# The layer norm of the convolution between the last value tiles, and the sample's convolution taps multiplied on ScalarE

## What is computed

```python
h = _rmsnorm(x, norm_mix_g)
q, k, v, iq, ik, iw, glu, ga, gc = jnp.split(h @ w_in, splits, axis=-1)
# branch A: selected sparse attention, 8 heads of 64; prompt and sample
attn_out = attention(q, k, v, iq, ik, iw, cache) @ w_attn_out
# branch B: convolution
ga_in, gb_in = jnp.split(glu, 2, axis=-1)
u = ga_in * jax.nn.sigmoid(gb_in)
u_full = jnp.concatenate([past_conv, u], axis=1)
c = causal_depthwise_conv(u_full, conv_dw_w)          # 31 taps, 512 channels
c = jax.nn.silu(_layernorm(c + conv_dw_b, conv_ln_g, conv_ln_b))
conv_out = c @ w_conv_out
x = x + (jax.nn.sigmoid(ga) * attn_out + jax.nn.sigmoid(gc) * conv_out) @ w_out
x = x + (jax.nn.silu(h2 @ w_ffn_gate) * (h2 @ w_ffn_up)) @ w_ffn_down   # h2 = rmsnorm(x)
```

## Time and profile before

| | us |
|---|---|
| median of 3 runs | 1997.33 |
| the profiled execution | 1996.86 |
| its span | 1995.1 |
| PE busy | 1872.1 (94%) |
| DVE busy | 1094.6 (55%) |
| ACT busy | 766.1 (38%) |
| POOL busy | 261.0 (13%) |

### The profile page before, as it was taken

How to read it: one execution, slowest core, us unless ns; L and a number is a source line. 1 busy time by engine, 2 the same in 40 slices (tenths; PEclk the granted TensorE clock), 3 DMA queues, 4 the chain that set the end, 5 groups by cost and what they waited for, 6 DMA issues and landing times.

```text
span 1995.1 us, 28433 instructions
## 1 busy us (share of the span) xinstructions
PE 1872.1 (94%) x11088; PEld 1647.4 (83%) x11088; DVE 1094.6 (55%) x1712; ACT 766.1 (38%) x1471; POOL 261.0 (13%) x287
## 2 busy tenths in 40 slices
PE   6977999999989966988999999999999999999998
PEld 3533799899989944656988889999999999999997
DVE  1045799897988977776454343333443333433333
ACT  2235655622367147765122233333223333333321
POOL 1001122122296022330000000000000000000000
PEclk9988999999999988999999999999999999999999
DMA  7110110332121323775321133333433333433332
GB/s 210 17 54 18 46 43 27 107 102 91 62 66 44 99 89 109 267 249 215 137 111 43 32 147 126 127 125 124 162 114 122 121 122 123 157 125 126 126 126 105
DMA packets 74236, 220.28 MB, mean 110 GB/s; under 512 B 14197, under 2 KB 25109, under 8 KB 65315
## 3 DMA queue, kind: packets, MB, share of 16 engines
q1 hardware_dynamic: 67963, 205.05, 30.3%
q10 hardware_dynamic: 6192, 14.16, 1.8%
HBM read 197.26 MB, written 21.89 MB: 110 GB/s over the span
## 4 chain that ended last, share of the span: by engine, by line
PE 56%; ACT 2%; DVE 1%; issue 1%; DVEq 0%; ACTq 0%
PE ps L653 17%; PE ps L652 17%; PE ps L651 17%; PE ps L881 1%; PE ps L858 1%; ACT buf L1260 1%; PE ps L915 1%; PE ps L900 1%; PE ps L871 1%; DVE buf L1571 1%; PE ps L971 0%; PE ps L887 0%; DVE buf L1396 0%; ACT buf L1250 0%; ACT buf L1302 0%
## 5 line engine op out<-in xcount | busy, mean ns | idle before, releaser
L651 PE MATMUL ps<-buf,buf 128*128 128x384 f32 (+2 forms) x2364 | 830.7, 351 | 17.3 <-DVE buf L1396 11.7
L653 PE MATMUL ps<-buf,buf 128*128 128x384 f32 (+2 forms) x2364 | 832.6, 352 | 0.0
L652 PE MATMUL ps<-buf,buf 128*128 128x384 f32 (+2 forms) x2364 | 830.7, 351 | 0.0
L651 PEld LDWEIGHTS ps<-buf,buf 128*128 128x128 f32 x2364 | 446.6, 189 | 43.2 <-DVE buf L1396 10.0
L652 PEld LDWEIGHTS ps<-buf,buf 128*128 128x128 f32 x2364 | 446.5, 189 | 24.3
L653 PEld LDWEIGHTS ps<-buf,buf 128*128 128x128 f32 x2364 | 446.2, 189 | 24.3
L1396 DVE TENSOR_TENSOR buf<-buf,buf 128x1024 fp32r<-128x1024 f32 (+4 forms) x245 | 335.6, 1376 | 184.2 <-ACT buf L1374 39.1
L1744 DVE TENSOR_TENSOR buf<-buf,ps 128x384 f32<-128x384 f32 x66 | 36.5, 553 | 403.1 <-PE ps L653 403.1
L1519 DVE SCALAR_TENSOR_TENSOR buf<-buf,buf,buf 128x1024 f32<-128x1024 f32 x240 | 197.4, 864 | 4.0
L1372 ACT ACTIVATE buf<-ps 128x384 f32<-128x384 f32 x66 | 32.5, 492 | 295.9 <-PE ps L653 295.9
L1374 ACT ACTIVATE buf<-buf 128x384 fp32r<-128x384 f32 x66 | 34.7, 525 | 282.1 <-DVE buf L1744 282.1
(11 more groups left out here) (182 smaller groups left out, 1746.5 us busy)
## 6 DMA issues: line engine op xcount, KB each, us to landing
buf<-in_w_ffn SPq DMA_DIRECT2D x67, 1024.0 KB, 5.6
buf<-in_w_ffn SPq DMA_DIRECT2D x66, 512.0 KB, 3.6
buf<-in_cache_k SPq DMA_DIRECT2D x16, 1024.0 KB, 7.3
buf<-in_cache_v SPq DMA_DIRECT2D x16, 1024.0 KB, 10.5
buf<-in_w_cols SPq DMA_DIRECT2D x24, 512.0 KB, 4.1
buf<-in_x SPq DMA_DIRECT2D x18, 512.0 KB, 3.7
gate_scr<-buf ACTq DMA_DIRECT2D x16, 576.0 KB, 4.8
buf<-gate_scr SPq DMA_DIRECT2D x16, 576.0 KB, 5.2
```

Of the source, the lines that this page charges most:

```text
L651: mm(dst, whi, xhi, start=start, stop=False)
L652: mm(dst, whi, xlo, start=False, stop=False)
L653: return mm(dst, wlo, xhi, start=False, stop=stop)
```

## The change

The diff makes five edits.

- The sample's part of the taps leaves VectorE's `conv_tap`. ScalarE multiplies the 128 sample tokens by each tap's weight (`sample_products(n)`, 24 parts of 6 or 5 taps), into one of two halves of `prod`. VectorE adds a part with one reduction over the taps and one addition (`sample_sum(n)`). Six parts stand in ScalarE's list between the evacuations of the last four column tiles (`in_columns`), 15 between the heads (`in_heads`), and 3 ahead of the value tiles. VectorE takes a sum behind every fifth tap, the first behind tap 8.
- The low parts of the weights now stand behind 20, 50, 66, 82, 98 and 114 taps, and the memset of `biasS` behind tap 118.
- The layer norm leaves the attention loop. On TensorE `layer_sums(0, c)` follows the value tiles t = 2, 3, 4 of f = 5 and `layer_sums(1, c)` the tiles 5, 6, 7. The value tiles of f = 5 go to banks 5 and 7 in turn, where they had three banks, and bank 6 is left for the sums. ScalarE's squares and root stand between its copies of the value tiles, with one buffer for the squares where there were two. VectorE does `less_mean` and `over_std` before the attention loop.
- The sample steps stand ahead of pairs 3, 7, 11, 15, 19, 23, 26 and 29, and the swish in steps 2 to 5.
- SP no longer waits for `conv_made` before it fetches a sixth of the weights, and three semaphores are merged into others.

```diff
-        sqc = take(2 * CT * G, o_w + 2 * HALF).rearrange("p (s j t) -> p s j t", s=2, j=CT)
+        sqc = take(CT * G, o_gmix).rearrange("p (j t) -> p j t", j=CT)
         acc = scoreS
+        prod = take(12 * P, o_gmix).rearrange("p (e d t) -> p e d t", e=2, d=6)
+        cuts = (0, 6, 11, 16, 21, 26, CK)
+        NPART = len(cuts) - 1
...
-        before = {10: 0, 13: 1, 16: 2, 19: 3, 22: 4, 25: 5, 27: 6, 29: 7}
+        before = {3: 0, 7: 1, 11: 2, 15: 3, 19: 4, 23: 5, 26: 6, 29: 7}
...
+            return bank(t // 2)[:, HW * (t % 2):HW * (t % 2) + HW] if f == 4 else bank(5 + 2 * (t % 2), HW)
...
             def layer_sums(k, c):
                 if k == 0:
                     pe.wait_ge(S("conv_made"), CT)
+                    pe.wait_ge(S("sample_summed"), CT * NPART)
...
+            for q in range(NQ):
+                project(q)
+                if 3 <= q < NQK + 3:
+                    turn(q - 3)
+                t = q - 5 * NT
+                if 2 <= t < 2 + NG:
+                    layer_sums(0, t - 2)
+                if 5 <= t < 5 + NG:
+                    layer_sums(1, t - 5)
...
+            def sample_products(n):
+                j, i = divmod(n, NPART)
+                if n >= 2:
+                    act.wait_ge(S("sample_summed"), n - 1)
+                else:
+                    act.wait_ge(S("mask_made"), NSEL)
+                for d in range(cuts[i], cuts[i + 1]):
+                    out = prod[:, n % 2, d - cuts[i]].rearrange("p (s q) -> p s q", s=NS)
+                    x = uSamp[:, j, :, d:d + QS]
+                    if d:
+                        l = ac(out, x, ACT.Copy, scale=cw[:, j, d:d + 1])
+                    else:
+                        l = ac(out, x, ACT.Identity, scale=cw[:, j, d:d + 1], bias=cb[:, j:j + 1])
+                    l.then_inc(S("sample_made"), 1)
+
+            in_columns = {(20, 2): 0, (21, 1): 1, (21, 2): 2, (22, 2): 3, (23, 1): 4, (23, 2): 5}
+            in_heads = {13 * k // 5: 6 + k for k in range(15)}
...
+            for t in range(NT):
+                values(t)
+                if t == 3:
+                    layer_norm(0, 0)
+                if 5 <= t < 5 + NG:
+                    layer_norm(1, t - 5)
+                    if t < 4 + NG:
+                        layer_norm(0, t - 4)
...
-                if 10 <= i < 10 + CT:
-                    swish(i - 10)
+                if 2 <= i < 2 + CT:
+                    swish(i - 2)
...
+            def sample_sum(n):
+                j, i = divmod(n, NPART)
+                dve.wait_ge(S("sample_made"), j * CK + cuts[i + 1])
+                src = prod[:, n % 2, 0:cuts[i + 1] - cuts[i]].rearrange("p d t -> p t d")
+                total, part = acc[:, NP:NTOK], newneg
+                if n:
+                    dve.wait_ge(S("sample_summed"), n)
+                if i == 0:
+                    l = ve.tensor_reduce(total, src, AX.X, ALU.add)
+                else:
+                    ch.link(ve.tensor_reduce(part, src, AX.X, ALU.add))
+                    dst = cT[:, j, NP:NTOK] if i == NPART - 1 else total
+                    l = ve.tensor_tensor(dst, total, part, ALU.add)
+                l.then_inc(S("sample_summed"), 1)
...
-            convolve(20)
-            qkv_low(0)
-            convolve(20)
-            for f in range(1, 6):
-                qkv_low(f)
-                convolve(14)
...
+            sums = iter(range(CT * NPART))
+            low_behind = {20: 0, 50: 1, 66: 2, 82: 3, 98: 4, 114: 5}
+            for m, (j, d) in enumerate(all_taps, 1):
+                conv_tap(j, d)
+                if m >= 8 and m % 5 == 3 and m < 123:
+                    sample_sum(next(sums))
+                if m in low_behind:
+                    qkv_low(low_behind[m])
...
+            for c in range(NG):
+                less_mean(c)
+            for j in range(NG + CT):
+                over_std(j)
```

More of the change, by code:

```diff
@@ L410, in qkv_bank @@
                 return bank(q % 4, HW)
-            return bank(t // 2)[:, HW * (t % 2):HW * (t % 2) + HW] if f == 4 else bank(5 + t % 3, HW)
+            return bank(t // 2)[:, HW * (t % 2):HW * (t % 2) + HW] if f == 4 else bank(5 + 2 * (t % 2), HW)
         @block.sync
@@ L939, in _ @@
                     turn_out(step(i - 4, "sample"))
-                if 1 <= i <= NG:
-                    layer_sums(0, i - 1)
-                if 4 <= i < 4 + NG:
-                    layer_sums(1, i - 4)
             def branches(i, first):
@@ L1143, in columns @@
                     l.then_inc(S("col_evac"), 1)
+                    if (t, c) in in_columns:
+                        sample_products(in_columns[t, c])
                 if not glu:
@@ L1217, in _ @@
                     qkv_high(q // NT + 1)
+                if q in in_heads:
+                    sample_products(in_heads[q])
             qkv_high(5)
-            for t in range(NT):
-                values(t)
+            for n in range(6 + len(in_heads), CT * NPART):
+                sample_products(n)
             def layer_norm(k, c):
@@ L1511, in conv_tap @@
             def conv_tap(j, d):
-                outs = (acc[:, 0:NP], acc[:, NP:NTOK].rearrange("p (s q) -> p s q", s=NS))
-                w = cw[:, j, d:d + 1]
-                for x, out in ((uT[:, j, d:d + NP], outs[0]), (uSamp[:, j, :, d:d + QS], outs[1])):
-                    if d == 0:
-                        ch.add(ve.tensor_scalar(out, x, w, cb[:, j:j + 1], ALU.mult, ALU.add))
-                    else:
-                        ch.add(ve.scalar_tensor_tensor(out, x, w, out, ALU.mult, ALU.add))
-                ch.wait()
+                x, w, out = uT[:, j, d:d + NP], cw[:, j, d:d + 1], acc[:, 0:NP]
+                if d == 0:
+                    ch.link(ve.tensor_scalar(out, x, w, cb[:, j:j + 1], ALU.mult, ALU.add))
+                else:
+                    ch.link(ve.scalar_tensor_tensor(out, x, w, out, ALU.mult, ALU.add))
                 if d == CK - 1:
-                    ve.tensor_copy(cT[:, j], acc).then_inc(S("conv_made"), 1)
+                    ve.tensor_copy(cT[:, j, 0:NP], out).then_inc(S("conv_made"), 1)
                     dve.wait_ge(S("conv_made"), j + 1)
+            def sample_sum(n):
[7 more added lines that the diff above has]
+                    l = ve.tensor_reduce(total, src, AX.X, ALU.add)
+                else:
+                    ch.link(ve.tensor_reduce(part, src, AX.X, ALU.add))
+                    dst = cT[:, j, NP:NTOK] if i == NPART - 1 else total
+                    l = ve.tensor_tensor(dst, total, part, ALU.add)
+                l.then_inc(S("sample_summed"), 1)
             all_taps = [(j, d) for j in range(CT) for d in range(CK)]
@@ L1530, in qkv_low @@
                 low(wqlo[f], wraw_[f], wqhi[f]).then_inc(S("qkv_split"), 1)
-            taps = iter(all_taps)
-            def convolve(n):
-                for j, d in itertools.islice(taps, n):
-                    conv_tap(j, d)
-            convolve(20)
-            qkv_low(0)
-            convolve(20)
-            for f in range(1, 6):
-                qkv_low(f)
-                convolve(14)
-            dve.wait_ge(S("qn_made"), 2 * NT)
-            dve.wait_ge(S("turn_made"), NQK)
-            ve.memset(biasS, 0.0).then_inc(S("biasS_zero"), 1)
-            convolve(CT * CK)
+            sums = iter(range(CT * NPART))
[6 more added lines that the diff above has]
+                    qkv_low(low_behind[m])
+                if m == 118:
+                    dve.wait_ge(S("qn_made"), 2 * NT)
+                    dve.wait_ge(S("turn_made"), NQK)
+                    ve.memset(biasS, 0.0).then_inc(S("biasS_zero"), 1)
+            for n in sums:
+                sample_sum(n)
             def less_mean(c):
```

43 lines of the change are left out of this document (14 added, 29 removed).

## The result

The changed kernel took 2023.85 us (median of 4 runs, 2023.12 to 2029.09), the kernel before 1997.12 beside it: a ratio of 1.014, 95% interval 1.0122 to 1.0157. It is slower by 26.7 us. The direction and the mechanism of the forecast (2015) hold; the size was 9 us short, which is the upper edge of its band (2008 to 2024) and a little nearer to the third rival (2031) than to 2015.

The account below looks back on a forecast made before the run. VectorE's convolution was taken to set when the attention starts. A first bias 38.5 us later, less 21 given back by the attention, made +17.5 on 1996.86, 2014.4, and 0.5 for the median: 2015; forecast band 2008 to 2024, range 1997 to 2031.

Parts of the forecast that it names:

- Short taps, -36: VectorE's convolution: removing 124 short taps saves 33.0 us, and 3 more from less waiting beside GpSimd.
- the port's term: Short taps' excess beside GpSimd: -11.4 us if it goes with them, 0 or +5 if inherited; taken as -3.
- 24 reductions, +21.0: VectorE's sums of ScalarE's products: 24 at 0.875 us with the gap, priced by element from a 576-element reduction.
- Additions +7.6: VectorE's convolution: 20 additions of 128 elements, each priced as a short tap, add 7.6 us.
- first stall +9.7: VectorE's first sum, behind tap 8, waits 9.7 us for ScalarE's first part; later parts have time.
- low parts' waits -11.7: VectorE's waits at the low parts for ScalarE's high parts, 11.7 us, vanish as these stand later; at worst half stays.
- The chain, 47.9: Layer norm ahead of the attention: sums, value tiles, root, reciprocals and products, from convolution's end at 699.6 to first bias at 747.5.
- The attention, -21: First bias to combination: 21 us shorter without the layer norm's work, bounds -30.5 and -10.
- ScalarE's products cost nothing: ScalarE's 124 products, 28 us, lie in a stage where it waits for GpSimd and TensorE, so add no time.
- The convolution doesn't get shorter: Third rival, chance 0.17: reductions at 1.28 us and port stalls end the convolution about 716; time about 2031.
- The attention takes everything back: Rival, chance 0.14: attention gives back 30.5 us instead of 21, convolution ends 5 us earlier; about 2000.
- Faster: Rival, chance 0.10: VectorE's list ends at 680, before TensorE reaches the sums at 681.4; about 1990.

Follow-up runs that it names:

- Experiment 5: The changed kernel with ScalarE's products laid out with the taps innermost, so that VectorE's reductions read in order: 2014.70 us, ratio 1.0093.
- the first try: The changed kernel with the layer norm back in the attention loop, products with taps innermost, low parts behind 20, 44, 58, 72, 86, 100 taps: 2006.16 us.
- experiment 1: The changed kernel with layer norm, sample-step table and swish as before, low parts behind 20, 40, 54, 68, 84, 98 taps: 2018.87 us.
- experiment 3: The changed kernel with the sample's taps back on VectorE and its convolution order of before; layer norm's new place and table stay: 2025.10 us, ratio 1.0144.
- experiment 4: The changed kernel with the table of sample steps of before and the swish in steps 10 to 13: 2020.98 us, ratio 1.0124.
- experiment 2: The changed kernel with layer norm, sample-step table and swish as before; taps on ScalarE and late low parts stay: 2007.04 us, ratio 1.0055.
- experiment 9: Two changed kernels: taps innermost, sums five taps later, low parts behind 20, 48, 64, 80, 96, 111; layer norm and table as before 1999.95 us, as changed 2012.94.

## Why the prediction was right, and where its size was off

- *The convolution bounds the start of the attention, and the sums now stand behind it.* Right: 9.36 us of TensorE's time ahead of the first group. It was half of the 18 forecast, since the third value tile was made at 697.7 instead of 681.4 and the list ended at 706.8 instead of 699.6. 13.8 of the tile's 16 us are TensorE's waits for low parts, 12.86 of them for the second. The prediction named the late low parts as covered by the wait, and they were.
- *Short taps, -36.* Without reductions, additions and waits the list shrank from 224.3 to 183.6 us, -40.7, which is within the bounds of the port's term.
- *24 reductions, +21.0.* This is the term that was mis-sized: 33.1 with the gaps, just above its upper bound of +32. The row chosen was of a reduction that costs 1.31 ns an element; the changed one reads with a stride and takes 2.04. Experiment 5 shows that the way of reading is the cause.
- *Additions +7.6, first stall +9.7, low parts' waits -11.7.* Measured 7.3, 8.7 with a later wait of 1.5, and -11.7. But the first try and experiment 1 show that the last term isn't independent: it holds only for low parts placed late.
- *How the errors add up.* +12.1 of the reductions and -4.7 of the taps partly cancel, and with the rest the list ends 7.2 us late. That the total lies only 9 us off is in part this luck.
- *The chain, 47.9.* Measured 47.5: first group 4.27 for 3.9, groups 5.42 apart for 5.58, the rest as read from the earlier trace rows.
- *The attention, -21.* Measured -19.0, and -21 in experiments 3, 4 and 5.
- *ScalarE's products cost nothing.* True for the time of this kernel, where the value tiles wait for the convolution anyway. But they kept ScalarE busy 41 us, not 28, and the lists of the two engines are tied to each other: in experiments 2 and 9 the tiles end 16 and 9 us later than before. In experiment 2, 13.8 of that are TensorE's waits for low parts; in experiment 9, 6 are its longer waits for the heads.
- *The signs of being wrong.* None came: the list ended between 682 and 712, no copy of a value tile held TensorE between the groups, and the attention, 202.6, lies between 192 and 211. Two of the signs expected didn't come either: reductions of 0.84 us and long taps at 1.28.
- *The rivals.* "The convolution doesn't get shorter" (716, 2031) was on the right side but too far: reductions as dear as it said and for its reason, the stride, port stalls less. "The attention takes everything back" falls, with -19 to -21 in every run. "Faster" needed a list that ends ahead of the third value tile, and no run reached that: in the twins of experiment 9 the streamed layer norm costs 13 us with a list that ends at 698.6, and TensorE was still waiting for it.

In one sum: from before's 1997 the layer norm's place is +28 (experiment 3); the taps with their low parts are +9 when they stand alone (experiment 2) and about nothing behind that wait. In all runs with the layer norm streamed, with lists that end between 698 and 713, the arithmetic of the chain is the same: 47.5 to 53 us put in front, 19 to 21 given back against the kernel before. What a list does that ends before the third value tile is not shown.

Left open: how much of the 9 us by which the tiles are late in experiment 9 is ScalarE's time for the products and how much is longer operations of GpSimd beside VectorE's; no kernel had the one without the other. Why the clock behind the first bias differs between kernels with the same attention stays open too.

## What to carry to other kernels

A chain of small dependent steps (sums, root, reciprocals) that ran among other work cost that work 19 to 21 us here; put in front of it as a block it cost its whole length, 47.5 us. Before an engine is relieved of work, look at what it waits for: 11.7 us of VectorE's list were waits for another engine, and moving five low parts by 3 to 8 taps and a memset by 8 took them out (1992.0), where moving 124 short taps to another engine gained nothing. When work in a list gets dearer, look at every instruction behind it that another engine waits for, and not only at the list's end: here it was the second low part, 138 us before the end, that held TensorE. And where a new operation is priced from a row of the same kind, compare the order in which both read, not only the number of elements.

## What the hardware showed that I had not expected

- A reduction over 5 x 128 f32 elements took 1304 ns reading with a stride of 128 elements and 820 ns reading them in order; 128 elements more cost 231 and 134 ns. The price didn't depend on the number of outputs (128 here, 9 in the row of before). ScalarE's products kept it busy 325 ns each written in order and 355 written with a stride of 6.
- The value tiles between the sums kept TensorE's clock up: groups of sums 2.74 us with them, most at 4.5 us without (granted clock 0.88 against 0.73 from the convolution's end to the first bias).
- When the short taps left VectorE, the long ones grew where GpSimd was busy (1386 ns against 1284), and the reductions, with one input, didn't (1315 against 1308).
- Two engines that wait for each other through small buffers lost 17.8 and 30.6 us in waits with low parts only 10 to 16 taps earlier; the time was 12 us longer (2018.87 against 2007.04).
